# Attention's small products in another order: scores change the partition half from product to product, products with v change the chunk first

## The reference, cut to what matters

```python
scores = einsum('bcqkgd,bcjkd->bckgqj', q, kb) * scale      # 64 deep, 64 or 128 keys
m = maximum(max(scores, -1), sink)
p = exp(scores - m)
probs = p / (sum(p, -1) + exp(sink - m))
o = einsum('bckgqj,bcjkd->bcqkgd', probs, vb)                # 64 or 128 keys deep, 64 wide
out = o.reshape(B, S, 2048) @ w_o
```

## Time and profile before

| what | value |
|---|---|
| median of 3 runs | 1939.12 us (1937.9 to 1939.57) |
| profiled execution, its own time | 1938.36 us |
| span of its trace | 1936.5 us |
| PE busy | 1919.9 us, 99% of the span |
| DVE busy, ACT busy | 1320.5 us, 964.4 us |
| score passes (line 488) | 128 |
| passes with v (line 510) | 64 |
| mean granted clock of PE | 0.996 |

### The profile page before, as it was taken

How to read it: one execution, slowest core, us unless ns; L and a number is a source line. 1 busy time by engine, 2 the same in 40 slices (tenths; PEclk the granted TensorE clock), 3 DMA queues, 4 the chain that set the end, 5 groups by cost and what they waited for, 6 DMA issues and landing times.

```text
span 1936.5 us, 26411 instructions
## 1 busy us (share of the span) xinstructions
PE 1919.9 (99%) x8641; PEld 1579.1 (82%) x8641; DVE 1320.5 (68%) x1819; ACT 964.4 (50%) x1303; POOL 6.2 (0%) x23
## 2 busy tenths in 40 slices
PE   9999999999999999999999999999999999999998
PEld 7777887888888888888888888878888888888886
DVE  7666588657855875686667986787568647855864
ACT  7665465434544443454554444654345435534542
POOL 0000000000000000000000000000000000000000
PEclk9999999999999999999999999999999999999999
DMA  7544556565565665556485565566565665555663
GB/s 256 166 148 175 192 164 199 202 198 178 192 213 175 193 209 194 182 185 208 144 277 174 185 205 190 169 197 209 193 192 181 210 196 181 197 196 174 195 206 109
DMA packets 188653, 368.40 MB, mean 190 GB/s; under 512 B 11434, under 2 KB 11572, under 8 KB 187828
## 3 DMA queue, kind: packets, MB, share of 16 engines
q1 hardware_dynamic: 187264, 360.75, 57.0%
q0 software_dynamic: 1040, 6.82, 1.0%
q10 hardware_dynamic: 292, 0.08, 0.0%
HBM read 365.52 MB, written 2.10 MB: 190 GB/s over the span
## 4 chain that ended last, share of the span: by engine, by line
PE 94%; DMA 2%; DVE 2%; ACT 1%; issue 1%; SPq 0%; DVEq 0%; ACTq 0%
PE acc L378 30%; PE acc L380 30%; PE acc L379 30%; DMA w_raw<-in_sgu_w_in 1%; DVE work L1009 1%; PE t L403 1%; DVE w_lo L978 1%; ACT w_hi L635 1%; PE scores L488 0%; PE o L510 0%; PE scores L380 0%; PE scores L378 0%; PE scores L379 0%; DMA w_raw<-in_mlp_w_up 0%; PE t L498 0%
## 5 line engine op out<-in xcount | busy, mean ns | idle before, releaser
L978 DVE TENSOR_TENSOR w_lo<-w_raw,w_hi 128x1024 fp32r<-128x1024 f32 x680 | 820.4, 1223 | 318.7 <-ACT w_hi L635 300.0
L635 ACT ACTIVATE w_hi<-w_raw 128x1024 fp32r<-128x1024 f32 x680 | 704.7, 1057 | 517.9 <-PE acc L380 442.3
L378 PE MATMUL acc<-w_hi,a_hi 128*128 128x512 f32 x1408 | 555.1, 394 | 5.1 <-ACT s L731 4.3
L379 PE MATMUL acc<-w_lo,a_hi 128*128 128x512 f32 x1408 | 549.5, 390 | 0.0
L380 PE MATMUL acc<-w_hi,a_lo 128*128 128x512 f32 x1408 | 549.4, 390 | 0.0
L378 PE MATMUL acc<-w_hi,b_hi 128*128 128x512 f32 x1280 | 499.1, 390 | 0.0
L380 PE MATMUL acc<-w_hi,b_lo 128*128 128x512 f32 x1280 | 498.1, 389 | 0.0
L379 PE MATMUL acc<-w_lo,b_hi 128*128 128x512 f32 x1280 | 498.0, 389 | 0.0
L1009 DVE STREAM_TRANSPOSE work<-s 32x256 f32<-32x256 f32 x576 | 251.2, 436 | 114.7 <-ACT s L766 104.9
L378 PEld LDWEIGHTS acc<-w_hi,a_hi 128*128 128x128 f32 x1408 | 265.1, 188 | 64.1 <-DVE w_lo L978 5.2
L380 PEld LDWEIGHTS acc<-w_hi,a_lo 128*128 128x128 f32 x1408 | 265.1, 188 | 56.1
(11 more groups left out here) (131 smaller groups left out, 500.0 us busy)
## 6 DMA issues: line engine op xcount, KB each, us to landing
w_raw<-in_mlp_w_up SPq DMA_DIRECT2D x256, 512.0 KB, 3.8
w_raw<-in_mlp_w_down SPq DMA_DIRECT2D x256, 512.0 KB, 4.3
w_raw<-in_sgu_w_in SPq DMA_DIRECT2D x64, 512.0 KB, 4.5
w_raw<-in_attn_w_qkv SPq DMA_DIRECT2D x40, 512.0 KB, 4.5
w_raw<-in_attn_w_o SPq DMA_DIRECT2D x32, 512.0 KB, 4.3
w_raw<-in_sgu_w_out SPq DMA_DIRECT2D x32, 512.0 KB, 4.5
gain<-in_norm_gains POOLq DMA_DIRECT2D x4, 1024.0 KB, 6.4
h<-in_x SPq DMA_DIRECT2D x8, 256.0 KB, 6.7
```

The source lines that it names most:

```text
L378: nc.tensor.matmul(bank[t][:, :], lhsT=x_hi[:, kb, tok], rhs=w1, start=(kb == 0), stop=False)
L379: nc.tensor.matmul(bank[t][:, :], lhsT=x_hi[:, kb, tok], rhs=w2, start=False, stop=False)
L635: nc.scalar.activation(w_hi[:, i % SLOTS, :], w_raw[:, i % RAW_SLOTS, :], ACT.Copy).then_inc(hi_made, 1)
L978: nc.vector.tensor_tensor(w_lo[:, i % SLOTS, :], w_raw[:, i % RAW_SLOTS, :], w_hi[:, i % SLOTS, :].bitcast(F32), ALU.subtract).then_inc(lo ...
```

## The change

Two loop nests on PE are turned over; no product, operand, wait or increment is added or removed.

```diff
@@ score(g, half)
-                    for e in range(2):
-                        for a in range(2):
+                    for a in range(2):
+                        for e in range(2):
                             row = slice(e * HD, (e + 1) * HD)
@@ weigh_v(g, half)
-                for i in (1, 0):
-                    c = 2 * half + i
-                    nk, _ = keys(c)
-                    for e in range(2):
+                for e in range(2):
+                    for i in (1, 0):
+                        c = 2 * half + i
+                        nk, _ = keys(c)
                         last = nc.tensor.matmul(ob[i][e * HD:(e + 1) * HD, 0:256], lhsT=v_cur[0:nk, (0, 0, 1, 2)[c], :],
                                                 rhs=pT[0:nk, i, e * 256:(e + 1) * 256], start=True, stop=True)
```

## The result

| | before | after |
|---|---|---|
| median of 16 runs each | 1937.98 us (1936.95 to 1939.57) | 1941.83 us (1938.27 to 1944.28) |
| profiled execution, its own time | 1938.36 us | 1942.39 us |
| span of its trace | 1936.5 us | 1940.6 us |

The ratio is 1.0017, with a 95% interval of 1.0011 to 1.0023. That is 3.3 us more (2.1 to 4.5), clear of no change; the means are 3.4 apart, the medians 3.85 and the two profiled executions 4.03. The forecast was +4.0, on the line of 0.2% (3.9 us) itself.

A forecast was written before the change was run, and what follows sets the result against it. PE's small attention products were taken to bound the kernel: -0.6 (scores) + 0 (products with v, half 1) + 4.6 (half 0) = +4.0 us, from 1939.12 to 1943.1 us, range 1938.6 to 1945.0.

The forecast's parts named there:

- What bounds: Attention on PE: its small products, 4.50 us a group and 18.0 in all, pass any gain or loss to the kernel.
- One sign of being wrong: After 180 us: the forecast is wrong if PE's lateness shortens or lengthens a wait there.
- Scores: Score products, both halves: alternating e saves 0.05 us of 1.14 and 0.10 of 1.19, 0.6 us over four groups.
- Products with v, half 1: Second half's products with v, all one shape: e = 1 still starts at once, 1.01 us stays, cost nothing.
- upper bounds of 0.27 and 0.70: Second half's products with v: delay if e = 1 started only with e = 0's second or fourth pass; at most 2.8 us.
- Products with v, half 0: First half's products with v: shape changes drain the array, four blocks replace two, 1.16 us more a group, 4.6 in all.
- (a): First half's products with v: shape change holds up only shared cells, three blocks; +1.7 us in all, 1940.8; chance 0.10.
- (b): Products with v: each array side changes shape for itself, no added cost; scores save 0.6, 1938.5 us; chance 0.12.
- (c): Queue too short or program order binds starts: second half's products with v cost more, scores save nothing; +7.4, 1946.5; chance 0.05.
- (d): Pairs are one product's two passes: two more shape changes in half 0; +0.6 to +1.2, 1939.7 to 1940.3; chance 0.04.
- The cases listed: Chances given: full drain 0.66, rivals 0.10, 0.12, 0.05 and 0.04, an unseen gain over 0.2% 0.03.

The follow-up runs named there:

- seven kernels: The changed kernel, 1941.83 us (ratio 1.0017 against the kernel before), and the six kernels of the follow-up experiments.
- long runs: Against the kernel before: e put outermost in the scores too, all eight passes of e = 0 and then e = 1; 1941.84 us against 1938.0, ratio 1.0023.
- three blocks: Against the kernel before: scores in the new order, half 0's products with v by (i, e) 10, 01, 00, 11; 1938.37 us against 1937.67, ratio 1.0006.
- scores alone: Against the kernel before: only the scores' loops turned over, products with v as before; 1936.89 us against 1938.0, ratio 0.9995.
- one shape: Against the changed kernel: chunk 0 padded with zeros to 128 keys; 1936.16 us against 1938.0 of the kernel before, ratio 0.9995.
- first four experiments: Scores alone, products with v reordered alone, one shape and long runs, run on one chip; ratios 0.9995, 1.0030, 0.9995 and 1.0023 against before.
- six kernels: In order: scores alone; products with v reordered alone (1.0030); one shape; long runs; three blocks; scores reordered plus chunk 0 padded, products with v as before (0.9994).

## Why the prediction was right

**What bounds.** That a microsecond of the small products is one of the kernel held in all seven kernels. The attention's length follows the sum of the steps within 0.25 us, from -1.2 to +4.6, and the medians of the whole times follow it within 1.0 us. PE has no gap in the stretch of attention of after either: busy 125.00 of 125.00 us from 60 to 185, at a granted clock of 1.00. One sign of being wrong was a wait of PE after 180 us that changes its length. Those waits (all for ACT) are 4.9 us in all before and 5.0 in after, the longest 2.2 and 2.5, so that nothing of size was hidden or added there. The prediction has PE waiting once, for ACT; PE's weight loads also waited 0.4 us once for DVE, while PE stayed busy.

**Scores.** Both savings came as worked out, 0.05 and 0.10, and the cause is shown and not only argued: the kernel of long runs, with the same products, grows to the 1.64 and 1.59 us that a depth of one running and three waiting passes gives, and its second side starts with the fifth pass of the first.

**Products with v, half 1.** Taken at nothing; 0.01. The upper bounds of 0.27 and 0.70 needed a shorter queue, which the long runs exclude for the scores and the row of 1.02, with both sides at 86.57, for these.

**Products with v, half 0.** Taken at 1.16 more, 2.32 in all; 1.14 more and 2.30. The last pass starts 1.99 after the first (77.72 to 79.71), forecast 2.0. The weak point in the argument was that no row of before showed a change of shape without shared cells. The third block of after and the second block of the kernel of three blocks now do. The rule of the Trainium skill, TensorEngine Tiling (Array Packing), section Key Properties, that changing the tiling mode drains the engine, agrees with these rows: 0.57 to 0.58 a block, of which 0.10 is the wait at the change.

**The rivals.** (a), a change of shape that holds up only shared cells, wanted 1.74 for after; it reads 2.30, and 77.47 in the kernel of three blocks refutes it directly. (b), each side changing for itself, wanted 1.16, against the same 2.30. (c) wanted half 1 at 1.28 or 1.7 and the scores' hole kept; half 1 reads 1.02 and the hole is gone. The strict order of starts that the Trainium skill, TensorE: Matmul & The Clock Gate, section The mechanism, states for matmuls doesn't hold across the two sides: in the kernel of long runs, by the reading given there, the ninth pass in order is in flight at 72.53 while the sixth to eighth have yet to start, and the step takes 1.64 us where strict order needs 1.97. (d), pairs made of the two passes of one product, falls by rows of after: the only product in a block has its passes 0.27 apart (79.44 and 79.71) and never together.

**Size and sign.** The forecast was +4.0, with 0.54 for no difference over 0.2% and 0.42 for slower. (The cases listed add up to 0.55, and to 0.03 for faster, where 0.04 is stated.) The steps gave 4.0 and the attention 3.75, the times 3.3 (2.1 to 4.5). What was less exact was not a term of the sum but what lies around it: 0.24 given back between the steps, and variation of a microsecond or two in the parts outside attention. On which side of 0.2% the ratio came to lie is luck: the mechanism that was forecast gave 4.0 against a line of 3.9. In absolute time the forecast of 1943.1 is 1.3 us above the measured 1941.83, and 1.1 of that is its starting point, the median of three runs of before (1939.12), where 16 runs give 1937.98.

## What to carry to other kernels

When small products use part of the array, write them in the order in which the halves alternate and equal shapes stand together: a product finds its partner only within a block of one shape, and only up to a few passes ahead. Where the shapes differ for a reason as small as a first chunk with half the keys, padding with zeros can be cheaper than the best order that was tried (1.01 us against 1.16), since a pass of 64 rows takes as long as one of 128: with either, the second pass of a block comes 0.27 after the first and the next shape 0.31 after that. To see such effects, compare the distances between starts in a stretch, not the program's time, in which 1.2 us of 1938 is lost.

## What the runs showed of the hardware that was not expected

The granted clock fell in some traces and not in others at the same place of the program. Behind the attention, where the MLP begins, PE waits 2.15 to 2.31 us for ACT's first tile; the wait ends between 294.6 and 300.2 us, by kernel. Windows of that wait and of the 3.4 us behind it, first of after, then of the kernel with the scores alone (stretch, length, PE busy, passes, clock, DMA share, GB/s):

```profile
296.79:299.10 2.31, 0.00 (x0) 1.00 0.73 217
299.10:302.50 3.40, 3.40 (x8) 0.51 1.00 357
```

```profile
293.30:295.49 2.19, 0.01 (x1) 1.00 0.82 235
295.49:298.89 3.40, 3.40 (x15) 1.00 0.98 345
```

After a wait of similar length the first is granted 1.2 GHz and makes 8 passes, and the second stays at 2.4 GHz and makes 15. The length of the wait doesn't decide it: the trace of before has the drop behind a wait of 2.20 us (0.51), the kernels of one shape and of three blocks don't have it there behind 2.28 and 2.26. The same wait comes a second time near 1275 us, with a drop in seven of the eight traces (0.53 to 0.68 over the 3.4 us behind it; 1.00 with the scores alone). What decides it stays open.

An estimate from these rows: at half the clock such a stretch costs about half of its length, 1.7 us, more than the padding and the scores' order saved together (1.2). Runs of one kernel differ along with their granted clock. The 28 runs of before that stand beside the first four experiments take 1939.4 us in the mean at a mean granted clock of 0.997 (9 runs), 1937.2 at 0.998 (14) and 1935.7 at 0.999 (4); one ran at 0.996. Compared at 0.998 alone, the six kernels differ from before by -0.8, +4.8, -1.4, +4.3, +1.5 and -0.9 us in the order of the experiments, where the sums of their steps are -0.60, +4.59, -1.13, +3.60, +1.68 and -1.20. So a gain of a microsecond that the time can't show can be looked for among runs of one clock. Each of these differences rests on 4 to 14 runs a side, and its standard error is 0.4 to 0.6 us.
